# One activation table for ScalarE, loaded by its first instruction

## The reference

```
def ada_norm(x, c, ada_w, ada_b, norm_g):
    mod = jax.nn.silu(c) @ ada_w + ada_b
    shift, scale, gate = jnp.split(mod, 3, axis=-1)
    h = rms_norm(x, norm_g) * (1 + scale[:, None]) + shift[:, None]
...
layer 0: q, k = rms_norm(q), rms_norm(k)          # 16 query heads, 2 key heads of 64
  A: p = exp(s - m); o = (p / (sum p + exp(sink - m))) v        # window of 128
  B: la = log_sigmoid(lr @ w_lr + b_lr) / 16; bcum = cumsum(la)  # 4 heads, chunks of 64
     q * exp(bcum), k * exp(-bcum), k * exp(blast - bcum)
     ob = rms_norm(ob)
  x + gate * ([oa * silu(ga), ob * silu(gb)] @ w_out)
layer 1: q, k rotated; 8 heads of retention with fixed decays
  o = rms_norm(o) * silu(g);  x + gate * (o @ w_out)
```

## Time and profile before

| | |
|---|---|
| timed, median of 3 runs | 3262.66 us (3262.16 to 3263.41) |
| profiled execution: span from first to last instruction | 3259.3 us |
| PE busy | 2980.1 us, 91% |
| DVE busy | 1125.9 us, 35% |
| ACT busy | 1062.7 us, 33% |
| mean granted clock of PE | 0.939 |

### The profile page before, as it was taken

One profiled execution on the slowest core, in us unless ns is written; L12 is line 12 of the kernel. 1 busy time (PEld: TensorE's weight loads), 2 busy tenths in 40 slices (PEclk: granted clock), 3 DMA queues, 4 the chain that ended last, 5 costly groups with the idle time before them and its releaser, 6 DMA issues.

```text
span 3259.3 us, 54092 instructions
## 1 busy us (share of the span) xinstructions
PE 2980.1 (91%) x22444; PEld 2733.4 (84%) x22444; DVE 1125.9 (35%) x1586; ACT 1062.7 (33%) x1500; POOL 238.3 (7%) x381
## 2 busy tenths in 40 slices
PE   4699997979789799799999999999999999889998
PEld 3388886869678699799989898998989898789998
DVE  1334443222222433433434233243434333433432
ACT  1235553332423322322425242341424242331221
POOL 1020000000000000001010010101010000101111
PEclk7599998989889799799999999999999999999999
DMA  8943331646446244325343343535344343546442
GB/s 302 289 141 110 110 110 42 187 126 196 130 145 198 78 137 134 92 80 176 92 156 102 123 137 96 160 92 166 93 140 125 113 144 89 191 120 193 119 126 72
DMA packets 525668, 442.58 MB, mean 136 GB/s; under 512 B 12239, under 2 KB 491877, under 8 KB 524928
## 3 DMA queue, kind: packets, MB, share of 16 engines
q1 hardware_dynamic: 485664, 300.30, 32.1%
q0 software_dynamic: 39824, 139.49, 12.4%
HBM read 370.36 MB, written 72.51 MB: 136 GB/s over the span
## 4 chain that ended last, share of the span: by engine, by line
PE 74%; ACT 7%; DVE 6%; issue 6%; DMA 6%; POOL 0%; ACTq 0%; DVEq 0%; SPq 0%; POOLq 0%
PE PJ L1379 58%; PE AD L1396 2%; DMA W_raw<-in_ada_w_even 2%; PE X L1761 2%; PE X L1361 2%; PE X L1755 2%; DMA W_raw<-in_w_in_even 1%; ACT W_hi L577 1%; PE X L1728 1%; PE X L1712 1%; PE X L1703 1%; ACT tiles L691 1%; DVE work L990 1%; DMA work<-in_state_gla 1%; ACT work L594 1%
## 5 line engine op out<-in xcount | busy, mean ns | idle before, releaser
L1379 PE MATMUL PJ<-act_hi,W_hi 128*128 128x272 f32 x5984 | 1765.3, 295 | 78.3 <-DVE act_lo L984 31.7
L1379 PE MATMUL PJ<-act_hi,W_lo 128*128 128x272 f32 x5984 | 1738.0, 290 | 3.7 <-issue 3.7
L1379 PE MATMUL PJ<-act_lo,W_hi 128*128 128x272 f32 x5984 | 1739.2, 291 | 0.0
L1379 PEld LDWEIGHTS PJ<-act_hi,W_hi 128*128 128x128 f32 x5984 | 1141.8, 191 | 136.9 <-issue 90.2
L1379 PEld LDWEIGHTS PJ<-act_lo,W_hi 128*128 128x128 f32 x5984 | 1143.6, 191 | 2.8
L1379 PEld LDWEIGHTS PJ<-act_hi,W_lo 128*128 128x128 f32 x5984 | 1140.9, 191 | 0.0
L939 DVE TENSOR_TENSOR W_lo<-W_raw,W_hi 128x2048 fp32r<-128x2048 f32 x187 | 428.1, 2290 | 506.8 <-ACT W_hi L577 500.5
L577 ACT ACTIVATE W_hi<-W_raw 128x2048 fp32r<-128x2048 f32 x187 | 356.6, 1907 | 263.0 <-PE PJ L1379 243.3
L581 ACT ACTIVATE tiles<-PJ 128x272 f32<-128x272 f32 (+1 forms) x224 | 87.8, 395 | 949.8 <-PE PJ L1379 949.1
L1279 DVE SCALAR_TENSOR_TENSOR W_raw<-W_raw,work,X 128x512 f32<-128x512 f32 x128 | 90.0, 744 | 144.1 <-PE X L1712 144.1
L1396 PE MATMUL AD<-W_raw,cs 128*32 128x256 f32 x1280 | 96.0, 451 | 35.9 <-DMA W_raw<-in_ada_w_even 22.7
(11 more groups left out here) (319 smaller groups left out, 2146.1 us busy)
## 6 DMA issues: line engine op xcount, KB each, us to landing
W_raw<-in_w_in_odd SPq DMA_DIRECT2D x96, 1024.0 KB, 6.0
W_raw<-in_ada_w_even SPq DMA_DIRECT2D x24, 2048.0 KB, 8.9
W_raw<-in_ada_w_odd SPq DMA_DIRECT2D x24, 2048.0 KB, 8.3
W_raw<-in_w_in_even SPq DMA_DIRECT2D x42, 1024.0 KB, 11.1
W_raw<-in_state_ret POOLq DMA_DIRECT2D x64, 512.0 KB, 7.1
out<-W_raw POOLq DMA_DIRECT2D x64, 512.0 KB, 3.2
W_raw<-in_w_out_odd SPq DMA_DIRECT2D x32, 1024.0 KB, 6.1
W_raw<-in_w_out_even SPq DMA_DIRECT2D x16, 1024.0 KB, 5.9
```

Source lines behind the costliest of these rows:

```text
L1379: last = mm(PJ[:, c, 0:HALF], w[:, par, k], x[:, k, c * HALF:(c + 1) * HALF], start=(k == 0 and a == 0), stop=(k == KT - 1 and a == 2))
```

## The change

More of the change, by code:

```diff
@@ L563, in _ @@
             A = nc.scalar.activation
+            act.preload_act_table_set("natural_log_exp_and_others")
             def wait_for(sm, value):
```

## The result

The changed kernel takes **3189.5 us** (median of 4 runs, 3184.7 to 3190.8); the kernel before, run beside it on the same chip, takes 3263.0 (3262.2 to 3265.8). That is 73.6 us less, where 72.1 had been forecast. The ratio of the medians is 0.9775; the ratio estimated from the runs of both is 0.9762, with an interval of 0.9749 to 0.9774. In the experiments that add lines they are higher still by as many.

What follows compares the result with a forecast made beforehand. TensorE, busy 91% of the span, bounds the kernel, so ScalarE time counts only where TensorE waits for it. 26.2+4.3+15.3+5.4+2.5+10.1+8.3 = 72.1 us off 3262.7 gives 3190.6 us, range 3176 to 3210.

Steps and rivals of the forecast that it cites:

- What a load costs a path: Read from an attention pair's Ln and Exp: 1.3 us for each load that stands on a path.
- Attention pairs: Eight pairs: 3.2 us saved in each of seven, 3.8 in the last, 26.2 us together.
- the pairs' second wait: TensorE's 1.4 us wait for the first head's probabilities (L1074) in each attention pair: 0.7 us of it is left.
- The norms: Two norms: 1.7 us saved in the first, where VectorE's W_lo split limits it, 2.6 in the second; 4.3 us.
- Linear attention: Some 5.1 us saved at each of three places between heads, 15.3 us, and 5.4 us after the last head.
- Retention: Retention heads: only the last two of ten loads per head reach TensorE, through an evacuation (L581); 2.5 us saved.
- Last head: Eighth retention head's norm and gates: TensorE's waits of 7.6 and 2.5 us for L1227 both go; 10.1 us.
- The clock: Stretches at 1.2 GHz behind attention-pair, modulation-tile and output-tile waits go with the waits; 8.3 us taken back.
- (a): Rival, whole kernel: every load counts, 150*1.3 = 195 us saved, 3068 us; chance 2%.
- (b): Rival, pairs and last head: VectorE takes ScalarE's place, 48 us saved with no clock coming back, 3215 us; chance 9%.
- (c): Rival, Exp and Ln on the path: the shared table is evaluated more slowly, at 0.6 us each 3287 us; chance 2%.
- (d): Rival, whole kernel: the loads stay or the engine refills its table unseen, 3262 us; chance 2%.

Runs made afterwards that it cites:

- moved split: Changed kernel with VectorE making the W_lo split before its wait for the query norm in the attention pairs, instead of after: 3188.3 us, ratio 0.9765.
- moved scores: Changed kernel with TensorE computing a pair's second-head scores before transposing the first head's probabilities, instead of after: 3187.9 us, ratio 0.9765.
- retention experiment: Changed kernel with table loads put back in the loop over retention heads 1 to 7 alone: 3193.6 us, ratio 0.9778.

## Why the prediction was right, and where it was not

- **What a load costs a path.** 1.3 us, read from one Ln and its Exp, carried every term. The Trainium skill's page "ScalarE: Activation LUTs", section "What ACT_TABLE_LOAD costs", adds a drain of 1.38 us to each load, with which the prediction put the sum at about 120 us. The traces don't agree: between Ln and Exp lie 1.32 us with a load of 1.28 and 0.03 without it, which leaves no room for a drain, and 73.6 us came.
- **Attention pairs**, 26.2 and 1.5 of clock: PE gained 22.8 us at the seven handovers (forecast 22.4), 1.5 by the clock, and 3.7 in and behind the last pair (3.8). Pitch 37.28 (37.4).
- **The step that failed** is the reason for the pairs' second wait: "the second wait hangs on a DVE chain that starts with L1058 and is 1.7 earlier, so 0.7 of it is left". That was the chain in the kernel before. The 0.84 us that stayed hang on PE's own scores, as the moved split and the moved scores showed. The size came out by luck, because split and scores end within 0.02 us of each other in the changed kernel. Who trusted the reason would have moved the split, for nothing.
- **The norms**, 4.3: the waits lost 1.7 and 2.5 us (the L1499 named there is a line of the attention heads; the norm's is L990). In the profile of the changed kernel PE kept only 0.9 at each; of the 1.9 us by which it is ahead when the pairs begin, 1.0 was there before the first norm. Why it kept less is not shown. The stretch at the lower clock in which the first wait lies ended hardly earlier, at 178.0 us where it was 178.9, which fits with wait that became slow matmuls. In the other traces without these loads the same matmuls took 1.2 to 2.4 us less than before in the first norm and 1.3 to 2.9 in the second.
- **Linear attention**, 15.3+5.4+3.0 of clock = 23.7: PE gained 22.6 there. The waits fell by 15.5 us at the three head changes and by 4.6 behind the last head; the rest is busy time. The wait for L1031 is gone altogether (forecast: under 2 us), so PE's jump to the loop's start did not take the 1.3 us back.
- **Retention**, 2.5: the wait of 2.5 us is gone, the stretch is 4.4 us shorter in this profile, and in others without loads by 1.9 or not at all. The term is as good as the row; the rest is the clock at the heads' state updates.
- **Last head**, 10.1 and 3.8 of clock: 57.6 to 71.4 = 13.8 us. The margin of 0.2 us held; no wait for the gates is left.
- **The clock**, 8.3: it came in the places named, 1.5 in the pairs, 3.0 at the head changes and 3.8 behind the last head. The longer low stretches, costed at nothing, moved by one to three us each, both ways, about as the prediction had said: the sample attention lost 1.3 us, a stretch ahead of the third head change 2.4, and the one behind the last head of linear attention gave 2.8.
- **The sum** is closer than its terms. In this profile the retention heads gave some 3 us more than forecast, the norms, the sample attention and the linear attention 1 to 2.5 us less each; that these nearly cancel, 71.4 for 72.1, is luck.

Of the rivals, (a) falls with the retention experiment, (b) with the pitch of 37.28 and the missing waits, (c) with the unchanged durations, (d) with the one load.

## What to carry to other kernels

Two functions that alternate in a chain can cost a table load each time although one table holds both: look in the trace for loads in equal numbers ahead of Ln and Exp, and count only those whose chain ends in a wait of the bounding engine, here 71 of 190 us. When a wait shrinks as forecast, still ask which of its inputs comes last now: two that end together look alike in the trace, and moving one of them is the way to tell. Price a wait of the matmul engine with the slow matmuls behind it, but take that part as a range.

## What the runs showed of the hardware

- Where the granted clock falls behind a short wait is not fixed by the wait. The same three waits of 1.0, 1.4 and 1.5 us per pair left one low stretch in eight pairs in the kernel before and three in the kernel with the loads put back there. Behind the waits of some 4 us between the heads of linear attention it came twice of three times, and three times of three.
- This sets what can be told from a run: ten kernels with the same instructions in the retention heads took 1475.2 to 1480.1 us there, and repeats of the changed kernel spread from 3181.2 to 3192.8 us.
- A load took 1283 ns for the set of both functions as for the sets it replaces, and none of the ACTIVATEs compared above became longer under it. No drain shows beside a load: 1.32 us from the end of Ln to the start of Exp with it, 0.03 without.
- A load need not be hidden because its Ln has to wait. In the kernel before, one load between two heads of linear attention ran 11 us ahead of its Ln, during the wait; in the second norm it began only when PE's row sum had ended, and its 1.28 us lay on the path. Why the two places differ is not shown.

```profile
684.26 1.28 ACT L588 ACT_TABLE_LOAD   x1
696.04 0.71 ACT L588 ACTIVATE work<-X,eps 128x544 f32<-128x544 f32 x1 [10.49 <-PE X L1389]
```

```profile
1316.60 1.28 ACT L588 ACT_TABLE_LOAD   x1 [2.49 <-PE X L1389]
```
